# Norm weights and the conv bias: from broadcast loads to a TensorE spread into PSUM

## The reference

```python
def rms_norm(x, g):
    y = xf * lax.rsqrt(jnp.mean(xf * xf, axis=-1, keepdims=True) + EPS)
    return y * g
# layer 0: h = rms_norm(x, mix_norm_e); x = x + attention_retention_mixer(h)
# layer 1: h = rms_norm(x, mix_norm_o); x = x + conformer_conv_module(h)
#          whose end is: return y @ w_pw2 + b_pw2
# every layer: h = rms_norm(x, ffn_norm[layer]); x = x + peer_ffn(h)
# at the end: rms_norm(x, final_norm)
```

## Time and profile before

| | us |
|---|---|
| median of 3 runs | 1603.08 (1602.32 to 1605.19) |
| profiled execution, its own time | 1604.01 |
| its span | 1602.3 |
| DVE busy | 1100.7 (69%) |
| PE busy | 1025.7 (64%) |
| POOL busy | 681.9 (43%) |
| ACT busy | 461.5 (29%) |
| DMA, bytes moved in the span | 622.17 MB, 388 GB/s |

### The profile page before, as it was taken

One profiled execution on the slowest core, in us unless ns is written; L12 is line 12 of the kernel. 1 busy time (PEld: TensorE's weight loads), 2 busy tenths in 40 slices (PEclk: granted clock), 3 DMA queues, 4 the chain that ended last, 5 costly groups with the idle time before them and its releaser, 6 DMA issues.

```text
span 1602.3 us, 20955 instructions
## 1 busy us (share of the span) xinstructions
PE 1025.7 (64%) x6998; PEld 540.2 (34%) x6998; DVE 1100.7 (69%) x2846; ACT 461.5 (29%) x1437; POOL 681.9 (43%) x566
## 2 busy tenths in 40 slices
PE   7999857555566585567746677645776547555654
PEld 7786424222333143223313344312333213111111
DVE  1745565877777877985567788899457977744444
ACT  2221313322223433323312334313323222222222
POOL 0002433444444454674444333574344444554551
PEclk9999878777777788878877889878888778787677
DMA  9046999999999999999999999999999999999994
GB/s 382 15 171 238 370 421 421 418 422 399 405 420 421 393 422 420 421 419 421 421 421 421 420 421 420 414 401 422 420 421 411 422 398 422 414 422 419 420 416 187
DMA packets 86739, 622.17 MB, mean 388 GB/s; under 512 B 9584, under 2 KB 10352, under 8 KB 12656
## 3 DMA queue, kind: packets, MB, share of 16 engines
q0 software_dynamic: 73728, 536.90, 81.0%
q1 hardware_dynamic: 12912, 84.01, 13.0%
HBM read 619.82 MB, written 1.05 MB: 387 GB/s over the span
## 4 chain that ended last, share of the span: by engine, by line
DMA 41%; PE 25%; DVE 25%; ACT 5%; DVEq 2%; issue 2%; ACTq 1%; POOL 0%; POOLq 0%
DMA ring<-experts_dram,idx_now 40%; DVE ring L968 10%; PE side L1390 9%; PE pm L1144 7%; PE side L1144 5%; DVE conv_buf L1015 4%; ACT diag_all L598 1%; ACT act_v L591 1%; DVE top_i L888 1%; DVE top_i L904 1%; DVE onehot L889 1%; DMA wbuf<-w_dram 1%; DVE best_i L913 1%; DVE diag_all L916 1%; DVE best_i L924 1%
## 5 line engine op out<-in xcount | busy, mean ns | idle before, releaser
L431 POOL DMA_INDIRECT ring<-experts_dram,idx_now x512 | 666.1, 1301 | 731.0 <-DMA ring<-experts_dram,idx_now 435.7
L1390 PE MATMUL side<-ring,diag_all 64*64 64x512 f32 x2048 | 631.0, 771 | 537.0 <-ACT diag_all L598 537.0
L968 DVE SCALAR_TENSOR_TENSOR ring<-ring,h_tok 128x1024 f32<-128x1024 f32 x512 | 606.4, 1222 | 148.6 <-DMA ring<-experts_dram,idx_now 141.9
L1390 PE MATMUL pm<-ring,diag_all 64*64 64x512 f32 x2048 | 630.8, 771 | 0.0
L1390 PEld LDWEIGHTS side<-ring,diag_all 64*64 64x64 f32 x2048 | 178.9, 173 | 940.3 <-ACT diag_all L598 570.6
L587 ACT ACTIVATE ge<-hb 128x4 f32<-128x4 f32 x128 | 26.3, 205 | 859.4 <-DVE ring L968 859.2
L1390 PEld LDWEIGHTS pm<-ring,diag_all 64*64 64x64 f32 x2048 | 177.8, 173 | 0.0
L598 ACT ACTIVATE diag_all<-ident,act_v 128x64 f32<-128x64 f32 x512 | 136.4, 336 | 10.5
L1015 DVE SCALAR_TENSOR_TENSOR conv_buf<-conv_buf,chan_sb 128x128 f32<-128x128 f32 x480 | 128.7, 342 | 0.0
L591 ACT ACTIVATE act_v<-ge,gates 128x1 f32<-128x1 f32 x512 | 109.0, 283 | 9.4 <-issue 0.7
L885 DVE MAX8 top_v<-side 128x8 f32<-128x128 f32 x64 | 15.2, 289 | 118.2 <-PE side L1365 118.1
(11 more groups left out here) (194 smaller groups left out, 836.6 us busy)
## 6 DMA issues: line engine op xcount, KB each, us to landing
wbuf<-wq_dram SPq DMA_DIRECT2D x28, 1024.0 KB, 9.8
wbuf<-w_dram SPq DMA_DIRECT2D x24, 1024.0 KB, 9.5
ring<-w_in_dram SPq DMA_DIRECT2D x5, 2048.0 KB, 22.5
wbuf<-w_o_dram SPq DMA_DIRECT2D x8, 1024.0 KB, 8.0
ring<-experts_dram,idx_now POOLq DMA_INDIRECT x512, 11.7
gain<-gains_dram SPq DMA_DIRECT2D x7, 512.0 KB, 13.7
ring<-w_in_dram SPq DMA_DIRECT2D x1, 1696.0 KB, 9.8
x_tok<-x_dram SPq DMA_DIRECT2D x2, 512.0 KB, 4.9
```

The costliest lines, as they stand in the source:

```text
L431: pool.indirect_dma_start(ring[:, r, :], None, table[layer], bass.IndirectOffsetOnAxis(idx_now[:, half, r:r + 1], 0)) \
L968: dve.scalar_tensor_tensor(out=ring[:, r, 0:D], in0=ring[:, r, 0:D], scalar=1.0, in1=h_tok[:, t, :], op0=ALU.mult, op1=ALU.mult, accum_out ...
L1390: step = pe.matmul(acc[half][c][j * HALF:(j + 1) * HALF, :], diag[rows, r % (2 * BATCH), :], ring[rows, r, D + c * COLS:D + (c + 1) * COLS ...
```

## The change

`gain` and its nine broadcast loads go. Instead `gain_rows`, six partitions of 1024, is loaded once at the start: the five norm rows and the bias row (two small DMAs where line 304 was). Whenever a norm needs its row on 128 partitions, PE makes it: `spread_gain(e)` is two products, each of a one-hot stationary matrix [6, 128] (a column of the identity, broadcast) with 512 columns of `gain_rows`, into PSUM at `gain_at(e)`. DVE reads it from there in line 709. There are eight spreads (norms 1 and 9 use the spread of norms 0 and 8; norm 3, which shared the buffer of norm 2, has its own now). The bias is not added by DVE any more: each of the four output products of a tile opens with a product of the bias row, so the sum holds it.

```diff
-GAIN_LOADS = [("norm", 0), ("norm", 2), ("norm", 4), ("bias", 0), ("norm", 5), ("norm", 6), ("bias", 1), ("norm", 7), ("norm", 8)]
-SAME_GAIN = {1: 0, 3: 2, 9: 8}
+GAIN_SPREADS = [0, 2, 3, 4, 5, 6, 7, 8]
+SAME_GAIN = {1: 0, 9: 8}
...
+            return side_flat[:, 0:1024] if e <= 2 else pm[:, 0:1024]
...
                 if t == 0:
-                    sp.dma_start(gain[:, 0, :], gains[0:1, :].broadcast_to([P, D])).then_inc(gain_loaded[0], 16)
+                    sp.dma_start(gain_rows[0:BIAS_ROW, :], gains).then_inc(gain_loaded, 16)
+                    sp.dma_start(gain_rows[BIAS_ROW:GAIN_ROWS, :], b2).then_inc(gain_loaded, 16)
...
-            load_gain("norm", 2)
...
-            load_gain("norm", 4)
...
-            load_gain("bias", 0)
...
-            load_gain("norm", 5)
...
-            load_gain("norm", 6)
...
-            load_gain("bias", 1)
...
-            load_gain("norm", 7)
...
-            load_gain("norm", 8)
...
-                dve.wait_ge(gain_loaded[g % 2], 16 * (g // 2 + 1))
+                dve.wait_ge(gain_ps, GAIN_SPREADS.index(SAME_GAIN.get(e, e)) + 1)
                 dve.scalar_tensor_tensor(out=h_tok[:, t, :], in0=x_tok[:, t, :], scalar=rstd[:, e:e + 1],
-                                         in1=gain[:, g % 2, :], op0=ALU.mult, op1=ALU.mult).then_inc(h_ready, 1)
+                                         in1=gain_at(e), op0=ALU.mult, op1=ALU.mult).then_inc(h_ready, 1)
...
             def conv_out(t):
-                g = GAIN_LOADS.index(("bias", t))
-                dve.wait_ge(gain_loaded[g % 2], 16 * (g // 2 + 1))
-                dve.tensor_tensor(x_tok[:, t, :], x_tok[:, t, :], gain[:, g % 2, :], ALU.add).then_inc(bias_added, 1)
-                dve.drain()
...
+            def gain_row(r):
+                return ident[0:GAIN_ROWS, r:r + 1].broadcast_to([GAIN_ROWS, P])
+            def spread_gain(e):
+                for c in range(2):
+                    last = pe.matmul(gain_at(e)[:, c * COLS:(c + 1) * COLS], gain_row(NORMS[e][0]),
+                                     gain_rows[:, c * COLS:(c + 1) * COLS], start=True, stop=True)
+                last.then_inc(gain_ps, 1)
...
             pe.wait_ge(const_ready, 2)
+            pe.wait_ge(gain_loaded, 32)
+            spread_gain(0)
             norm_h_t(0)
...
             logit_products(1)
+            pe.wait_ge(projected_added, 2)
+            spread_gain(2)
             for c in range(2, 4):
                 output_product(0, c)
...
                 if p and i == 0:
+                    spread_gain(2 * p + 2)
                     pe.wait_ge(x_ready, (0, 3, 5, 7)[p])
...
-                product(dst, lambda k: z_t[:, k, :], lambda k: w[:, k, :]).then_inc(w2_ps, 1)
+                pe.matmul(dst, gain_row(BIAS_ROW), gain_rows[:, c * WCOLS:(c + 1) * WCOLS], start=True, stop=False)
+                for k in range(KD):
+                    last = pe.matmul(dst, z_t[:, k, :], w[:, k, :], start=False, stop=(k == KD - 1))
+                last.then_inc(w2_ps, 1)
...
+                if (i, b) == (5, 1):
+                    pe.wait_ge(x_ready, 2 * t + 4)
+                    spread_gain(2 * t + 5)
                 if (i, b) == (5, 2):
                     norm_h_t(2 * t + 5)
...
+                if (i, b) == (1, 2):
+                    pe.wait_ge(projected_added, 8)
+                    spread_gain(3)
                 if (i, b) == (1, 3):
                     norm_h_t(3)
```

More of the change, by code:

```diff
@@ L51 @@
 FIN = 8
-GAIN_LOADS = [("norm", 0), ("norm", 2), ("norm", 4), ("bias", 0), ("norm", 5), ("norm", 6), ("bias", 1), ("norm", 7), ("norm", 8)]
-SAME_GAIN = {1: 0, 3: 2, 9: 8}
+GAIN_SPREADS = [0, 2, 3, 4, 5, 6, 7, 8]
+SAME_GAIN = {1: 0, 9: 8}
+GAIN_ROWS = 6
+BIAS_ROW = 5
 X_OF_NORM = [0, 0, 1, 2, 3, 4, 5, 6, 7, 8]
@@ L111, in hybrid_decoder_trunk_kernel @@
         h_t = sb("h_t", [P, KD, P])
-        gain = sb("gain", [P, 2, D])
+        gain_rows = sb("gain_rows", [GAIN_ROWS, D])
         wbuf = sb("wbuf", [P, WBUF, KD, WCOLS])
@@ L237, in hybrid_decoder_trunk_kernel @@
         const_ready = sem("const_ready")
-        gain_loaded = [sem(f"gain_loaded{i}") for i in range(2)]
+        gain_loaded, gain_ps = sem("gain_loaded"), sem("gain_ps")
         norm_root, h_ready, h_t_ps, h_t_ready = sem("norm_root"), sem("h_ready"), sem("h_t_ps"), sem("h_t_ready")
         x_ready = sem("x_ready")
-        bias_added = sem("bias_added")
         proj_ps = sem("proj_ps")
@@ L284, in norm_at, with gain_at @@
             return side_flat[:, 1024:2048] if e == 2 else pm[:, 1024:2048] if e == 1 else pm[:, 0:1024]
+        def gain_at(e):
+            return side_flat[:, 0:1024] if e <= 2 else pm[:, 0:1024]
         def head_slot(h):
@@ L314, in _ @@
             sp.dma_start(chan_sb[:, :], chan).then_inc(small_loaded, 16)
[L316 to L323, removed]
             def multiplied(n):
@@ L706, in norm @@
                 dve.drain()
-                g = GAIN_LOADS.index(("norm", SAME_GAIN.get(e, e)))
-                dve.wait_ge(gain_loaded[g % 2], 16 * (g // 2 + 1))
+                dve.wait_ge(gain_ps, GAIN_SPREADS.index(SAME_GAIN.get(e, e)) + 1)
                 dve.scalar_tensor_tensor(out=h_tok[:, t, :], in0=x_tok[:, t, :], scalar=rstd[:, e:e + 1],
-                                         in1=gain[:, g % 2, :], op0=ALU.mult, op1=ALU.mult).then_inc(h_ready, 1)
+                                         in1=gain_at(e), op0=ALU.mult, op1=ALU.mult).then_inc(h_ready, 1)
             dve.sem_inc(s_read, 2)
```

## The result

After the change the kernel takes 1606.38 us (median of 22 runs), against 1603.55 us for the kernel before (22 runs beside them). The ratio is 1.0024, with a 95% interval of 1.0016 to 1.0032: slower by 0.24%; the median lies 10.5 us above the forecast. One of the 22 runs before took 2132 us and counts in no ratio (without it their median is 1603.45). The profiled execution took 1612.19 us, 5.8 over its own median, so its late passes hold some time that the median run doesn't; I lean on its order of events and on differences that other traces repeat.

A forecast was written before the change was run, and what follows sets the result against it. After about 170 us DMA at 421 GB/s was taken as the bound, before that a chain: -8.7 us for seven loads and +1.5 for norm 2's spread, -7.2 in all, gave a median of 1595.9 us, range 1592 to 1601.

The forecast's parts named there:

- Part 7: Spreads for norms 3, 5, 7 stand behind a batch: DVE waits about 5 us each, costed at nothing, uncovered 15 us.
- Part 1: Broadcast loads that go: seven after 170 us, 1.245 us each on a full DMA, save 8.7 us.
- D: Rival: DVE's waits at norms 3, 5 and 7 starve the gather queue; up to 1610.9 us; chance 0.09.
- C: Rival: bytes are not time, slots set pass lengths, the loads give nothing back; 1604.6 us; chance 0.17.
- Part 2 and 3: Kernel start: smaller loads cost nothing; norm 0's spread costs 0 to 1.2 us, taken as 0.
- rival B: Start: the early spread wakes PE, speeding the transposes and first ckv product; 1592.3 us; chance 0.12.
- Part 5: DVE's norms read the weight row from PSUM: a PSUM operand costs nothing.
- Part 6: Spreads 4, 6, 8 at pass starts fit in PE's 9.14 us idle: nothing; uncovered, 2 us each.
- Part 8: Bias moved from DVE to PE: DVE's wait in `conv_out` grows under 1 us, twice, hidden; nothing.

The follow-up runs named there:

- e7: e1 with norm 2's spread left out, norm 2 multiplying by x in place of its weight row; ratio 0.9969.
- e8: e1 with norm 2's spread made twice, four products in place of two; ratio 0.9978.
- e10: Kernel before with all loads, plus a dead spread and DVE's wait for it at norms 5 and 7 alone; 1604.30 us, ratio 1.0000.
- e5: Kernel after with only norm 3's spread one batch earlier on PE, those of norms 5 and 7 still late; 1603.37 us, ratio 0.9993.
- e2: Kernel before without its eight later broadcast loads, all norms and the bias reading the first row; 1597.05 us, ratio 0.9961.
- e12: The same file as e1, measured again; 1597.99 us, ratio 0.9965.
- e1: Kernel after with the spreads of norms 3, 5 and 7 each one batch earlier on PE; 1597.28 us, ratio 0.9972.
- e6: Kernel after with only the spreads of norms 5 and 7 one batch earlier, norm 3's still late; 1603.51 us, ratio 0.9995.
- e4: Kernel after plus seven dead broadcast loads, at the old places, into a buffer nobody reads; 1610.80 us, ratio 1.0038.
- e3: Kernel before with all loads, plus dead spreads at the change's late places and DVE waiting for them in norms 3, 5 and 7; 1609.48 us, ratio 1.0031.
- e11: e9 with three dead spreads in place of one, so norm 3 waits 11.1 us; 1616.35 us, ratio 1.0081.
- e9: Kernel before with all loads, plus a dead spread and DVE's wait for it at norm 3 alone; 1608.86 us, ratio 1.0036.

## Why the prediction was wrong, step by step

**The bound.** "So after about 170 us time is bytes" is the root of both errors. I read the DMA share and the rate, which say that DMA is full, and took from it that nothing else binds. I also called the window of the earlier trace rows the one where DVE comes closest, but the earlier trace rows, inside pass 0, shows DVE busy 13.33 of 14 us (95%). (The strip's ceiling is 422 and not 421; nothing hangs on that.) The chain of waits of the kernel before says otherwise; by line, first in pass 0 (170 to 530 us), then in pass 1 (540 to 890 us), then in pass 2 (895 to 1245 us):

```profile
by line: PE side L1390 27.3%; DVE ring L968 17.8%; PE side L1144 14.3%; PE pm L1144 3.0%; issue 2.9%; DVE top_i L888 2.2%; DVE top_i L904 2.1%; DVE onehot L889 2.0%; ACT act_v L591 1.8%; ACT diag_all L598 1.8%; DVE best_i L913 1.7%; DVE dia
```
```profile
by line: DMA ring<-experts_dram,idx_now 72.0%; PE side L1390 6.0%; DVE ring L968 5.5%; issue 2.3%; PE side L1144 2.1%; POOL ring L431 1.0%; ACT act_v L591 0.8%; ACT diag_all L598 0.7%; DVE top_i L888 0.7%; DVE onehot L889 0.6%; DVE top_i L9
```
```profile
by line: DVE ring L968 21.2%; DVE conv_buf L1015 18.0%; DMA ring<-experts_dram,idx_now 17.3%; PE side L1390 7.6%; PE pm L1144 3.7%; DMA wbuf<-w_dram 3.1%; ACT diag_all L598 2.6%; ACT act_v L591 2.5%; ACT L609 2.2%; PE side L1144 2.1%; issue
```

In pass 0 no gather is among the costliest lines of the chain: PE, DVE and ACT hand each other the work of each batch, and free slots just fast enough for DMA to look full. Two limits lie close together there, and the one that the strip shows isn't the one that binds. In pass 1 the gathers are the chain; in pass 2 DVE leads it. The Trainium skill (Perfetto Trace Analysis, section "Identifying the Most-Contended Engine") says to find the engine with the highest occupancy, judging DMA by how much of the memory's rate it uses, and to optimize that one first. That names DMA in pass 0 as well; the runs don't agree, since loads taken from it there gave 0.0 us.

**Part 7 failed:** "I cost it at nothing", since five gathers in flight cover 12.5 us and "DVE ... makes it up in about four picks". The three waits were there as forecast (4.82, 5.3 and 3.80 us for "about 5"). But at norm 3 DVE didn't make it up: the chain of PE, DVE and ACT had no slack to give, and a wait of 4.8 us cost 5.4. Five traces have this wait in its plain size, and pass 0 takes 308.2 to 308.8 us in them; eight, with e7 and e8, don't have it and show 302.7 to 302.9. My reading of this: the gathers in flight bridge a late slot once, and where the chain runs no faster than DMA the delay is not won back.

At norms 5 and 7 the argument held as long as the loads were in: e10 costs nothing. Without the loads it doesn't: the interval of e5 (0.9979 to 1.0008) lies above that of e2 (up to 0.9975), meets that of e12 (up to 0.9979) at its end and overlaps only e1's (up to 0.9994), and its passes 1 to 3 take 1060.7 against 1052.7 and 1050.5 in e1 and e12. Pass 1 takes 356.4 us in e5 and in the kernel after, and 353.0 in four traces that have neither the loads nor the wait (e2, e7, e8, e12); two more of that kind, e1 and e6, show 357.6 and 358.7, and nothing on record explains them. The chain of pass 1 in the kernel after is no longer DMA:

```profile
by line: DVE ring L956 23.2%; DVE conv_buf L1003 18.0%; PE side L1390 15.1%; PE side L1139 4.2%; PE pm L1424 3.6%; ACT act_v L580 3.2%; ACT diag_all L587 3.1%; DMA wbuf<-w_dram 2.8%; issue 2.1%; ACT L598 1.8%; PE pm L1139 1.7%; ACTq L583 0.
```

The account that fits is that these passes last as long as the longer of two paths: the saved bytes shortened the one, the waits lengthened the other, and the second took over. The runs show that the two parts of the change don't add up; the two paths themselves are read from the chains and from no run of their own.

**Part 1 was mis-sized:** the two loads in pass 0 are worth 0, in two pairs of traces (e2 and before, e4 and after). The five behind it give 6.0 us in e2's trace for 6.2, with a scatter of 2.2 between traces of one file, and e2's median is 6.3 under before. So minus 8.7 should have been about minus 6.2.

**The sum over the profiled executions** shows where the difference of 15.4 us (1612.2 for 1596.8) went: +5.4 for norm 3; +2.5 for the two worthless loads; -1.3 at the start of the passes, where the third index copy came 0.2 us late and not 1.5; and +8.7 in passes 1 to 3, which were to give 6.2 and lost 2.4 (1058.9 for 1056.5). That leaves 0.1. In medians the miss is 10.5; the rest is that this profiled execution lies 5.8 over its median where the forecast allowed 0.9, most likely in the last term. The last term would then be some 3.8, and passes 1 to 3 of the median run still gained 2 to 3 us: an estimate, as no trace of that run exists. How the last term divides between norms 5 and 7 and the longer bias wait isn't settled: single traces of the same file differ there by 2.2 us (e1 and e12).

**The rivals.** D, the slower side, was right in kind, and had a chance of 0.09. Its price was about right too: it said the gain is eaten when 7 of 15 us come through, and norm 3 with the two others gave 9.1 by the medians. Its condition, "at most two gathers in flight", was the wrong one; at norm 3 POOL had just issued four gathers (268.25 to 273.36), DMA went on at 414 to 422 GB/s until 281, and only then did the rate fall. My reading is that the slack of the pass's chain decides. C was right for one pass of four.

**What held.** Part 2 and 3: ACT had x's first tile at 4.85 instead of 4.47, the spread ran from 5.42 to 9.17, and DVE began norm 0 at 9.22 instead of 8.84, 0.4 us within "0 to 1.2":

```profile
4.85 1.28 ACT L442 ACT_TABLE_LOAD   x1 [4.85 <-DMA x_tok<-x_dram]
5.42 3.75 PE L1132 MATMUL side<-gain_rows,ident 6*128 6x512 f32 x4 [5.42 <-DMA gain_rows<-b_dram]
9.22 1.28 DVE L697 SCALAR_TENSOR_TENSOR h_tok<-x_tok,rstd,side 128x1024 f32<-128x1024 f32 x1
10.55 3.67 PE L1122 MATMUL pm<-ident,h_tok 128*128 128x128 f32 x16 [1.38 <-DVE h_tok L697]
```

The transposes took 3.67 us behind the spread as they had without it (3.65), against rival B. Part 5: line 697 with its row in PSUM takes 1.28 us, as line 709 with it in SBUF. Part 6: e4, with the true spreads and the bias, and e3, without them, agree within error (1.0038 and 1.0031). Part 8: DVE's wait in `conv_out` grew from 31.6 us (4 times) to 38.5, more than the forecast's "under 1 us, twice", though e4 against e3 doesn't show it in the time.

## What to carry to other kernels

A DMA share near 1 doesn't say that other engines have slack: read the chain of waits pass by pass before you price a saved byte or a new wait, because in pass 0 a saved byte gave nothing and a wait was paid in full, while behind it the savings counted and the same waits were free until the bytes were gone. A helper product that an engine with an in-order list makes for a neighbour belongs ahead of the batch it would queue behind; moving three spreads ahead by one batch turned 2.8 us lost into 6 us gained.

## What was not expected of the hardware

**A spread that cost next to nothing.** The spread of norm 2 took its 1.98 us of PE at 103.44, and the output products behind it began at 105.34 instead of 103.07. But the first index copy stayed at 138.81 (138.61 before). The time came back at 129 us, in four products of 512 columns that wait for ACT. First the kernel without the spread (e7, window and timeline), then e12 with it; the last three columns of a window are the granted clock, the DMA share and GB/s.

```profile
129.00:132.00 3.00, 3.00 (x4) 1.10 (x4) 2.63 (x9) 0.31 (x2) 0.00 (x0) 0.52 0.00 0
127.23 5.40 PE L1285 MATMUL pm<-ring 128*128 128x512 f32 x8 [1.95 <-ACT ring L518]
```
```profile
129.00:132.00 3.00, 3.00 (x20) 2.26 (x19) 2.63 (x9) 1.32 (x3) 0.00 (x0) 1.00 0.02 5
126.77 3.70 PE L1284 MATMUL pm<-ring 128*128 128x512 f32 x8 [1.95 <-ACT ring L518]
```

Without the spread the granted clock fell to about half, the 1.2 GHz level, behind the idle 1.95 us, and the products took 5.40 us; with it the clock stayed at the full 2.4 GHz and they took 3.70. The 1.7 us between them nearly equal the spread. Six traces without the spread show 5.40 (clock 0.50 to 0.85 in this window), six with one show 3.70 (clock 1.00). One doesn't fit: e11 has no such spread and shows 3.70. Up to there it runs as e10 does, within 0.01 us (125.38 and 125.39 for these products), so something besides the spread decides whether the clock falls. With the spread made twice the clock fell earlier, about 1 us behind the four products of six rows, and the output products took 8.86 us for 7.17, so e8 lost 3.2 us at the first index copy instead of the 1.7 of a second spread:

```profile
108.00:111.00 3.00, 3.00 (x9) 2.41 (x8) 1.95 (x1) 0.00 (x0) 0.00 (x0) 0.54 0.00 0
```

Here and in e11 at 257 us it fell while PE had no pause, during or just behind products of six rows. Why it falls in the one case and not in the other stays open; no run set it apart from the shift in time that each spread brings. The lesson for the working is that a PE term of 2 us near an idle stretch has a range of its own size, in either direction.

**The start varies by 2 us by itself.** ACT read the first ckv product, behind a wait of 3.83 us, at 18.6 to 19.0 us in e4, e5, e9, e10, e11 and e12 and at 20.4 to 21.2, behind 5.28 to 5.96 us, in the other eight traces, with the early spread and without it in both groups. What rival B counted on does happen, but the change doesn't cause it.
